# Three attentions of a four-layer transformer kernel: the first two steps' scores, maxima and exponentials issued ahead of the layer's last projections

## The reference, cut to what matters

```
layer 1  diff: softmax(q0 k0) - lambda * softmax(q1 k1), 8 heads, causal
layer 2  nsa:  compressed, selected and windowed attention, 16 heads, causal
layer 3  mla:  q = rms(h Wq) Wuq, k|v = rms(h Wkv) Wukv, rope on 32 of 96 rows,
               softmax(q k / sqrt(96)) v, 8 heads; beside it a gated linear attention
layer 4  gqa:  q, k = rope(rms(h W)), softmax(q k / 8) v, 16 heads, 4 key heads
layers 1, 2:   32 experts of width 256, top 2;  layers 3, 4: 16 experts of width 1024,
               each takes its 32 best tokens (expert choice)
```

## Time and profile before

| | |
|---|---|
| time of 3 runs, median (lowest to highest) | 2169.41 us (2169.15 to 2170.88) |
| the profiled execution: its own time / its span | 2167.44 us / 2165.7 us |
| TensorE busy / weight loads busy | 82% / 51% of the span |
| VectorE / ScalarE / GpSimd busy | 21% / 18% / 0% |
| bytes moved | 716 MB, mean 331 GB/s |
| mean granted TensorE clock | 0.902 of full |

### The profile page before, as it was taken

One profiled execution on the slowest core, in us unless ns is written; L12 is line 12 of the kernel. 1 busy time (PEld: TensorE's weight loads), 2 busy tenths in 40 slices (PEclk: granted clock), 3 DMA queues, 4 the chain that ended last, 5 costly groups with the idle time before them and its releaser, 6 DMA issues.

```text
span 2165.7 us, 31101 instructions
## 1 busy us (share of the span) xinstructions
PE 1768.7 (82%) x13297; PEld 1104.2 (51%) x13297; DVE 445.5 (21%) x1064; ACT 396.5 (18%) x908; POOL 0.6 (0%) x5
## 2 busy tenths in 40 slices
PE   7989999999999988998987566565889976556667
PEld 5858665568576655686853131221577642222214
DVE  3342311123632111225211000000244210000002
ACT  3131311122623111224211010000223310000001
POOL 0000000000000000000000000000000000000000
PEclk9999999999999999999998777877999987876868
DMA  9976899986648999934599999999932899999996
GB/s 358 289 260 253 350 382 402 379 247 228 230 143 338 373 394 383 310 124 137 182 408 421 421 421 422 421 421 422 340 136 99 322 413 422 421 421 421 421 421 267
DMA packets 185024, 716.00 MB, mean 331 GB/s; under 512 B 28428, under 2 KB 95928, under 8 KB 114360
## 3 DMA queue, kind: packets, MB, share of 16 engines
q1 hardware_dynamic: 184172, 713.48, 84.2%
q10 hardware_dynamic: 716, 0.53, 0.1%
HBM read 826.16 MB, written 1.05 MB: 382 GB/s over the span
## 4 chain that ended last, share of the span: by engine, by line
PE 55%; DMA 33%; DVE 5%; SPq 3%; ACT 2%; issue 2%; ACTq 0%; DVEq 0%; POOLq 0%
DMA ring<-in_w 27%; PE ps L1009 18%; PE ps L1446 7%; PE ps L1356 6%; DMA ring<-in_moe_w_up 5%; PE ps L1490 3%; PE ps L1366 3%; PE ps L1384 3%; PE ps L986 2%; PE ps L1340 2%; PE ps L1151 2%; SPq L826 1%; DMA ring<-in_moe_w_gate 1%; SPq L892 1%; PE ps L1078 1%
## 5 line engine op out<-in xcount | busy, mean ns | idle before, releaser
L1446 PE MATMUL ps<-ring,ptb 128*32 128x512 f32 x1936 | 319.9, 810 | 196.5 <-DMA ring<-in_w 182.8
L1446 PEld LDWEIGHTS ps<-ring,ptb 128*32 128x32 f32 x1936 | 82.6, 143 | 419.4 <-issue 403.7
L1490 PE MATMUL ps<-ring,pb 128*32 128x512 f32 x1024 | 146.1, 725 | 75.8 <-DMA ring<-in_w 74.5
L1009 PE MATMUL ps<-xT,ring 128*128 128x256 f32 (+2 forms) x640 | 138.0, 385 | 0.9 <-ACT xT L1768 0.4
L1490 PEld LDWEIGHTS ps<-ring,pb 128*32 128x32 f32 x1024 | 39.2, 129 | 175.3 <-issue 172.9
L1009 PEld LDWEIGHTS ps<-xT,ring 128*128 128x128 f32 (+2 forms) x640 | 114.0, 185 | 24.6 <-issue 8.2
L2540 DVE TENSOR_TENSOR kT<-pb,ps 128x1024 f32<-128x1024 f32 x8 | 9.8, 1221 | 522.0 <-ACT pb L1957 522.0
L1009 PE MATMUL ps<-oT,ring 128*128 128x256 f32 x512 | 114.0, 381 | 2.0 <-DVE oT L2297 1.1
L1356 PE MATMUL ps<-ring,vt 128*32 128x256 f32 x1536 | 93.9, 403 | 17.9 <-DMA ring<-in_moe_w_up 14.5
L1009 PE MATMUL ps<-hT,ring 128*128 128x256 f32 x480 | 104.6, 380 | 1.5 <-ACT hT L1768 1.5
L1009 PEld LDWEIGHTS ps<-oT,ring 128*128 128x128 f32 x512 | 96.2, 190 | 15.6 <-DVE oT L2297 2.0
(11 more groups left out here) (463 smaller groups left out, 1931.4 us busy)
## 6 DMA issues: line engine op xcount, KB each, us to landing
ring<-in_w SPq DMA_DIRECT2D x370, 1024.0 KB
ring<-in_moe_w_gate SPq DMA_DIRECT2D x96, 1024.0 KB
ring<-in_moe_w_up SPq DMA_DIRECT2D x96, 1024.0 KB
ring<-in_moe_w_down SPq DMA_DIRECT2D x96, 1024.0 KB
ring<-in_ada_w SPq DMA_DIRECT2D x48, 1024.0 KB
ring<-in_diff_w_in SPq DMA_DIRECT2D x12, 1024.0 KB
ring<-in_w_o SPq DMA_DIRECT2D x8, 1024.0 KB
ring<-in_ple_gate_w SPq DMA_DIRECT2D x8, 1024.0 KB
```

The source lines that it names most:

```text
L1009: last = mmul(o, l, r, start=start, stop=stop)
L1446: last = mmul(ps[32 * j:32 * j + 32, 2 * a + h, :], xg[:, k, 32 * j:32 * j + 32], w[j][2 * k2 + h], start=(k == 0), stop=(k == C - 1))
L1490: last = mmul(ps[32 * j:32 * j + 32, 6 + h, :], hidT2[:, c, 32 * j:32 * j + 32], w[j][2 * c2 + h], start=(c == 0), stop=(c == C - 1))
```

## The change

In diff, mla and gqa (nsa keeps its order) the first two steps leave the attention:

- TensorE: `scores` of steps 0 and 1 stand ahead of the layer's last projections: ahead of the last 2 of diff's 12 jobs, ahead of the last 4 of mla's 10 small jobs (two key jobs, two value jobs), ahead of the last 2 of gqa's 8 jobs (its value jobs). Each `scores` now waits for the ropes that it needs, not for all of them.
- VectorE: the maxima of both steps and the normalising of step 0 (`begin`) stand ahead of the attention; in mla ahead of the last rope.
- ScalarE: `exps` of steps 0 and 1 stand between the evacuations of the last projections.
- In mla the rope of the shared key rows and their copy into `kT` (L2788) move ahead of `partition_norms(1)`.
- In gqa the pieces of the norms and ropes are put inside the projections (`inside`, called after the first half of a job), the norms run one job further ahead, and the last rope moves into the attention, behind transposes(1) on TensorE and behind neg_max(3) on VectorE; transposes(0) waits for the last norm. Banks of the last norms and ropes change (`spread_bank`, `rope_bank`). ScalarE loads the table for roots once more after the exponentials of step 1, and the one for exponentials after it.
- `p` of diff's first two steps lies in `sqb` and `rt`, since `hT` is still read by the last projections.
- `att_go` counts 1 (nsa), 2 (mla's keys copied), 3 and 4: SP's two waits for 3 and 4 now end after mla's last rope and evacuation, and after gqa's last rope, inside its attention. `attention` on TensorE waits for the evacuation of the layer's last projection instead of `att_go`.

```diff
+        def spread_bank(i):
+            return {12: 6, 13: 7}.get(i, 5 + i % 2)
...
+        def ropes_needed(x):
+            c = x["n"] - first_step[x["kind"]]
+            return {"diff": 5 + c // 2, "nsa": r_even, "mla": r_even + 2 + c, "gqa": r_odd + max(4, 3 + c // 2)}[x["kind"]]
+
+        def rope_bank(i):
+            if i < r_end - 2:
+                return 2 + i % 2
+            return 6 if i == r_end - 2 else o_user[st_span["gqa"][1]["n"]] % 2
...
         def p_of(x):
+            if x["n"] < 2:
+                return (sqb, rt)[x["n"]][:, 0:1024].rearrange("p (u n) -> p u n", u=2)
             return soft[x["kind"]][x["n"] % 2].rearrange("p (u n) -> p u n", u=2)
...
-            def project(js):
+            def project(js, between=None):
...
+                        if between and x == 0:
+                            between()
...
+            def scores(x):
+
+                n, b = x["n"], 2 + 2 * (x["n"] % 2)
+                pe.wait_ge(S("rope_done"), ropes_needed(x))
+                if x["kind"] == "mla":
+                    pe.wait_ge(S("att_go"), 2)
+                    await_need(pe, ("job", ev_kv + n - first_step["mla"]))
...
                     pe.wait_ge(S("p_ready"), n + 1)
+                    if n == first_step["gqa"]:
+                        pe.wait_ge(S("rope_done"), r_end - 1)
+                        pe.wait_ge(S("pn_done"), 14)
...
-                pe.wait_ge(S("att_go"), {"diff": 1, "nsa": 2, "mla": 3, "gqa": 4}[name])
-                scores(xs[0])
                 if name == "nsa":
...
+                else:
+                    await_need(pe, ("job", ph[{"diff": "diff_out", "mla": "even_out", "gqa": "odd_out"}[name]] - 1))
...
+                    if name == "gqa" and i == 1:
+                        rope(r_end - 1)
...
-            project(span["diff"][4:])
             pe.wait_ge(S("consts_rest"), 16)
+            project(span["diff"][4:10])
+            for x in st_span["diff"][:2]:
+                scores(x)
+            project(span["diff"][10:])
             attention("diff")
...
-            project(range(ev_uq, ph["even_out"]))
+            project(range(ev_uq, ev_kv + 2))
+            for x in st_span["mla"][:2]:
+                scores(x)
+            project(range(ev_kv + 2, ph["even_out"]))
             attention("mla")
...
             project(span["odd"][0:2])
-            for s in range(6):
-                pn_sums(2 + s)
-                project(span["odd"][s + 2:s + 3])
-                ropes_until(r_odd + s)
-                pn_spread(8 + s)
-            ropes_until(r_end)
+            pn_sums(2)
+
+            def inside(s):
+                if s == 0:
+                    pn_spread(8)
+                pn_sums(3 + s)
+                if s:
+                    rope(r_odd + s)
+
+            for s in range(4):
+                project(span["odd"][2 + s:3 + s], lambda s=s: inside(s))
+                pn_spread(9 + s)
+                if s == 0:
+                    rope(r_odd)
+            for x in st_span["gqa"][:2]:
+                scores(x)
+            project(span["odd"][6:7])
+            pn_sums(7)
+            rope(r_odd + 4)
+            project(span["odd"][7:8])
+            pn_spread(13)
             attention("gqa")
...
-            evacuate(span["diff"][4:])
+            evacuate(span["diff"][4:10])
+            for x in st_span["diff"][:2]:
+                exps(x)
+            evacuate(span["diff"][10:])
...
+            evacuate(range(ev_uq, ev_kv + 2))
+            exps(st_span["mla"][0])
+            evacuate(range(ev_kv + 2, ev_kv + 4))
+            exps(st_span["mla"][1])
+            evacuate(range(ev_kv + 4, ph["even_out"]))
...
+            for x in st_span["gqa"][:2]:
+                exps(x)
+            evacuate(span["odd"][6:7])
+            pn_roots(7)
+            func(misc[:, 57:58], eps_col, ACT.Exp)
+            evacuate(span["odd"][7:8])
...
+            def begin(name):
+                neg_max(st_span[name][0])
+                neg_max(st_span[name][1])
+                normalise(st_span[name][0])
...
             gla_stage()
+            ropes_until(r_even + 1)
+            V.tensor_copy(kT[64:96, :, :], kpe[64:96, :].rearrange("p (o t) -> p o t", o=1).to_broadcast([32, C, T]))\
+                .then_inc(S("att_go"), 1)
             partition_norms(1)
+            ropes_until(r_odd - 1)
+            begin("mla")
             ropes_until(r_odd)
...
+            begin("gqa")
+            pn_inverse(7)
+            ropes_until(r_end - 1)
+            partition_norm(13)
+
+            def last_rope():
+                ropes_until(r_end)
+                V.memset(misc[:, 58:59], 0.0).then_inc(S("att_go"), 1)
+
+            attention("gqa", turn=last_rope)
```

More of the change, by code:

```diff
@@ L1018, in rope @@
                     pe.wait_ge(S("rope_done"), i - 1)
+                if i == r_end - 1:
+                    await_need(pe, ("job", ph["odd_out"] - 1))
                 rr = slice(r0, r0 + rows)
-                mmul(ps[rr, 2 + i % 2, 0:n * T], rot[rr, rr], buf[rr, :], start=True, stop=True)\
+                mmul(ps[rr, rope_bank(i), 0:n * T], rot[rr, rr], buf[rr, :], start=True, stop=True)\
                     .then_inc(S("rope_mm"), 1)
[L1023 to L1026, removed]
             def pn_sums(b):
@@ L1174, in attention @@
                 ada = ADA_STEP.get(name, ())
[L1176 to L1195, removed]
                 def transposes(x):
@@ L1799, in partition_norms, with exps @@
                 pn_roots(b)
+            def exps(x):
+                n, p, b = x["n"], p_of(x), 2 + 2 * (x["n"] % 2)
+                act.wait_ge(S("nm_ready"), n + 1)
+                if n >= 2:
+                    act.wait_ge(S("t_done"), n - 1)
+                for tt, cols in enumerate([slice(0, P), slice(P, P + T)] if x["causal"] else
+                                          [slice(0, T), slice(T, 2 * T)]):
+                    for u in range(2):
+                        a = 2 * tt + u
+                        last = func(p[:, u, cols], ps[:, b + u, cols], ACT.Exp, bias=stat(x, "bias")[:, a:a + 1],
+                                    scale=x["scale"], accum_out=stat(x, "sum")[:, a:a + 1])
+                last.then_inc(S("exp_done"), 1)
             def attention(name):
@@ new lines, in normalise @@
+            def normalise(x):
+                p, r = p_of(x), stat(x, "coef")
+                dve.wait_ge(S("exp_done"), x["n"] + 1)
+                link(V.reciprocal(r, stat(x, "sum")))
+                if x["kind"] == "diff":
+                    link(V.tensor_tensor(r[:, 1:4:2], r[:, 1:4:2], coef[:, 0:2], ALU.mult))
+                    for tt, cols in enumerate((slice(0, P), slice(P, P + T))):
+                        last = V.tensor_scalar(p[:, 0, cols], p[:, 0, cols], r[:, 2 * tt:2 * tt + 1], None, ALU.mult)
+                    link(last)
+                    for tt, cols in enumerate((slice(0, P), slice(P, P + T))):
+                        last = V.scalar_tensor_tensor(p[:, 1, cols], p[:, 1, cols], r[:, 2 * tt + 1:2 * tt + 2],
+                                                      p[:, 0, cols], ALU.mult, ALU.add)
+                else:
+                    if x["coef"] is not None:
+                        r3 = r.rearrange("p (t u) -> p t u", t=TT)
+                        link(V.tensor_tensor(r3, r3, x["coef"], ALU.mult))
+                    for tt, cols in enumerate((slice(0, P), slice(P, P + T)) if x["causal"] else
+                                              (slice(0, T), slice(T, 2 * T))):
+                        w = cols.stop - cols.start
+                        rb = r[:, 2 * tt:2 * tt + 2].rearrange("p (u o) -> p u o", o=1).to_broadcast([P, 2, w])
+                        last = V.tensor_tensor(p[:, :, cols], p[:, :, cols], rb, ALU.mult)
+                last.then_inc(S("p_ready"), 1)
@@ L2794, in _ @@
             norm(6)
[L2795 to L2802 removed]
+            pn_inverse(2)
+            partition_norm(8)
+            pn_inverse(3)
+            partition_norm(9)
+            ropes_until(r_odd + 1)
+            for s in range(3):
+                pn_inverse(4 + s)
+                ropes_until(r_odd + 2 + s)
+                partition_norm(10 + s)
+            begin("gqa")
[4 more added lines that the diff above has]
+                ropes_until(r_end)
+                V.memset(misc[:, 58:59], 0.0).then_inc(S("att_go"), 1)
+            attention("gqa", turn=last_rope)
             residual("odd_out", 3)
```

125 lines of the change are left out of this document (53 added, 72 removed).

## The result

| | time, median (lowest to highest) | profiled execution: time / span |
|---|---|---|
| before | 2170.14 us (2169.15 to 2171.57, 4 runs) | 2167.44 / 2165.7 us |
| after | 2152.22 us (2149.18 to 2155.92, 4 runs) | 2149.18 / 2147.4 us |

The ratio is 0.9915, 95% interval 0.9899 to 0.9931: 17.9 us faster by the medians, 18.4 by the ratio (15.0 to 21.9). The forecast was 11.3 us and 2158.0 us, its range ended at 2152.5, 0.3 us above the median. Of the forecast's cases it is the rival *the clock stays up*, with somewhat more in each start than that rival had.

What follows compares the result with a forecast made beforehand. TensorE's work and waits were taken to bound the kernel; gains of 1.8 (diff), 4.2 (mla) and 5.3 (gqa) made 11.3 us, so 2156.1 us profiled, plus 1.97 for the median: 2158 us, range 2152.5 to 2165.5.

Steps and rivals of the forecast that it cites:

- the clock stays up: Rival: the new order never drops TensorE's clock in the three starts; gain 14.3 us, 2155 us; chance 0.2.
- What bounds the kernel, and that a gain arrives: TensorE's work plus its waits bound the time; a microsecond won in an attention's start arrives at the kernel's end.
- The gain doesn't arrive: Rival: earlier transfers bind the streamed stretches of layers 3 and 4; only diff's 1.8 us stay, 2167.5 us; chance 0.1.
- The deduction for the lower clock: Remaining waits in the starts lower TensorE's clock, costing up to 1.6 us in diff, 3.0 in mla, 2.5 in gqa.
- The sizes at full clock: Gains in the three starts if the clock stays at its upper level: diff 2.4 us, mla 5.4, gqa 6.5.
- The sum: Gains of the three starts, 1.8 + 4.2 + 5.3 = 11.3 us; full-clock bound 14.3, lower-clock bound 7.8.
- New waits: TensorE waits: diff about 2 us for normalise(1), mla 1.2 and 1.7 around value jobs, gqa some 2 for normalise(2).
- The waits come back further on: Rival: early steps run into VectorE in gqa, evacuations in mla; gain 6 us with lower clock, 2163 us; chance 0.2.
- Tables: ScalarE's table loads in gqa priced at 1.28 us; at the skill's 2.66 us the sum would be 0.8 us worse.
- Cover of the key rope: Mla's key rope and copy cost nothing when moved into VectorE's idle time; without that cover, 2.9 us.

Runs made afterwards that it cites:

- the parts alone: Three kernels, each the kernel before with the new order in only one attention: diff ratio 0.9979, mla 0.9974, gqa 0.9948.
- the repeat: The changed kernel, unaltered, measured again beside the kernel before: ratio 0.9925 (0.9912 to 0.9939), 2154.72 us.

## Why the prediction fell short

**What bounds the kernel, and that a gain arrives: right.** Experts2 of layer 3 kept its length and its transfers started earlier with it. *The gain doesn't arrive* is refuted by the parts alone.

**The deduction for the lower clock: the step that failed.** The prediction took values between its two bounds (diff 1.8 of 0.8 to 2.4, mla 4.2 of 3.0 to 5.4, gqa 5.3 of 4.0 to 6.5), 3.0 us less in all, "With the clock down after waits of 1.2 and 1.7 us" in mla and the like in diff and gqa. None of it was paid: in every start with the new order, 27 of them in eleven profiles, the clock was 1.00, with waits up to 2.83 us. The prediction rested this on one wait of 1.97 us that had cost the clock; that row is real and its price of 1.6 us was right, but the same wait costs nothing in half of the profiles. In the nine starts with the old order and no filling the clock fell each time, behind a wait of about 4 us in mla and behind two or three waits of 0.9 to 2.4 us in diff and gqa. What separates these from the waits of the new order stays open. The Trainium skill ("TensorE: Matmul & The Clock Gate", What's actually happening) says that activity releases the throttle; the filled waits agree, with 1.00 in three starts that had 0.72 to 0.78.

**The sizes at full clock: too small by 2.0 us.** Diff 2.6 for 2.4. Mla 6.1 for 5.4: scores and first maximum came when forecast (9.0 and 11.0 us after the first query job), but two evacuations behind the exponentials were counted as 1.3 us and took 1.07, and exponentials of step 1 ended 0.4 us earlier, so the last evacuation ended at 18.2 us instead of 18.9. Gqa 7.6 for 6.5: the scores started within 0.3 us of the forecast, spread(13) ended 0.65 us ahead of it, and normalise(2) began 1.2 us ahead, so half of the difference is in the jobs and half in VectorE's steps behind them.

**The sum.** 11.3 + 3.0 (no lower clock) + 2.0 (sizes) = 16.3 us in the starts, as the stretches show; with the 1.1 us behind diff, for which the forecast had no term, it is 17.4, and the timed 18.4 and 16.3 us lie on both sides of it. The range ended 16.9 us below the median it started from, because it allowed 2.5 us over the full-clock bound. That the median lies 0.3 us outside of it is chance, since the repeat's 2154.72 us lie inside. That the gain is larger than the forecast's 11.3 us is not chance: 11.3 lies below both intervals, 15.0 to 21.9 and 13.2 to 19.1.

**New waits: right in place, shorter than forecast.** Normalise(1) in diff (1.44 us for 2), evacuations around mla's value jobs (0.43 and 1.27 for 1.2 and 1.7), the last rope in gqa (1.57 for 2). Of the two waits above 1 us that were to stand around mla's value jobs only one did, and gqa's 0.82 us for normalise(1) was not named. *The waits come back further on*: the waits came, but they were already in the forecast's sum, and the steps behind them kept their pace of 3.1 us.

**Tables.** The three loads in gqa last 1.28 us. Behind the two added ones the next activation follows directly (1598.01 after 1596.72, 1599.59 after 1598.30); the first is followed by a wait for the maximum. No wait of TensorE ends on a load. The Trainium skill ("ScalarE: Activation LUTs", What ACT_TABLE_LOAD costs) puts a switch at 2.66 us. This trace does not agree: the activation at 1598.01 ends at 1598.28, and the next one starts 1.31 us later with a switch in between.

**Cover of the key rope: right**, and priced right: 2.7 us measured without it, 2.9 forecast.

## What to carry to other kernels

When a chain over three engines stands at the start of a phase, its head can be issued inside the dense work ahead of it. Most of the gain is idle time: filling the waits alone, which brought the clock back, gave only 4 of 16 us in the starts. Read for each moved step what now stands behind it on the in-order engine: moving normalise(1) and the last rope by one place was worth another 4.3 us in the starts. One row in which a wait cost the clock is no price for all waits: look for the same wait in other executions before charging it.

## Hardware behaviour that I had not expected

- The same wait of 1.97 us, after the same work, is followed by the lower TensorE clock in 7 of 14 profiles (6.35 to 6.41 us instead of 4.72 to the next transposes), while waits of 2.79 and 2.83 us in gqa and mla were followed by none.
- Filling TensorE's waits with products whose result nobody reads raised the granted clock of three starts from 0.72 to 0.78 to 1.00 and made the kernel 8.5 us (5.6 to 11.3) faster with nothing brought forward in the program.
- Unchanged code differs between executions: the streams by up to 6 us, and a stretch of layer 2 by 5 us (192.2 to 197.3) with the same idle time and a granted clock of 0.98 to 0.95. Effects of 2 us could only be read from stretches of the profile that the change touches.
